# Packing the buffers of an encoder kernel without padding, and loading a scaled identity instead of computing it

## The reference

```python
DN_ALPHA = (2 * DEPTH) ** 0.25
...
# layer 0:  h = norm(ALPHA * h + mixer(h)); h = norm(ALPHA * h + swiglu(h))
# layer 1:  h = norm(ALPHA * h + mixer(h)); h = norm(ALPHA * h + experts(h))
```

## Time and profile before

| | |
|---|---|
| runs | 1726.48, 1728.03, 1727.89 us; median 1727.89 |
| profiled execution | 1726.48 us, span 1724.6 us from its first to its last instruction |
| PE busy | 1650.9 us, 96% of the span |
| DVE busy | 1353.5 us, 78% |
| ACT busy | 944.0 us, 55% |
| DMA | 444.23 MB, 258 GB/s over the span |
| mean granted clock of TensorE | 0.958 of full speed |

### The profile page before, as it was taken

One profiled execution on the slowest core, in us unless ns is written; L12 is line 12 of the kernel. 1 busy time (PEld: TensorE's weight loads), 2 busy tenths in 40 slices (PEclk: granted clock), 3 DMA queues, 4 the chain that ended last, 5 costly groups with the idle time before them and its releaser, 6 DMA issues.

```text
span 1724.6 us, 18678 instructions
## 1 busy us (share of the span) xinstructions
PE 1650.9 (96%) x7674; PEld 1306.7 (76%) x7674; DVE 1353.5 (78%) x1443; ACT 944.0 (55%) x943; POOL 56.4 (3%) x39
## 2 busy tenths in 40 slices
PE   6998989999999998899999999999999999999995
PEld 4665748988858764788888888888888888888883
DVE  6879456765665945598898998888988989888996
ACT  4312315654310232477777776777777767777772
POOL 0111000000011100000000000000000000000000
PEclk9978989999998978799999999999999999999997
DMA  7221152743433114598988998998989989989870
GB/s 311 98 98 49 74 212 86 270 182 147 173 145 147 49 73 182 208 371 344 375 351 339 372 353 346 366 362 337 364 348 354 361 356 356 360 330 374 350 305 26
DMA packets 40459, 444.23 MB, mean 258 GB/s; under 512 B 4400, under 2 KB 4528, under 8 KB 7216
## 3 DMA queue, kind: packets, MB, share of 16 engines
q1 hardware_dynamic: 39216, 438.78, 65.2%
q10 hardware_dynamic: 1152, 4.19, 0.6%
HBM read 437.71 MB, written 5.24 MB: 257 GB/s over the span
## 4 chain that ended last, share of the span: by engine, by line
PE 84%; DVE 10%; ACT 4%; issue 1%; DMA 0%; DVEq 0%; SPq 0%; ACTq 0%
PE bank L1075 33%; PE bank L1096 15%; PE bank L981 7%; PE bank L583 4%; PE bank L990 3%; PE bank L800 3%; PE bank L587 3%; PE bank L1039 2%; PE bank L753 1%; PE bank L1083 1%; DVE ring_lo L1962 1%; DVE ring_lo L2086 1%; ACT ex_up_hi L1353 1%; PE bank L726 1%; PE bank L1059 1%
## 5 line engine op out<-in xcount | busy, mean ns | idle before, releaser
L1962 DVE TENSOR_TENSOR ring_lo<-ring,ex_up_hi 128x2048 fp32r<-128x2048 f32 x224 | 512.8, 2290 | 50.9 <-ACT ex_up_hi L1353 50.7
L1353 ACT ACTIVATE ex_up_hi<-ring 128x2048 fp32r<-128x2048 f32 x224 | 429.1, 1916 | 115.7 <-PE bank L1075 108.0
L1075 PE MATMUL bank<-ex_up_hi,ex_x_hi 128*128 128x512 f32 x896 | 363.0, 405 | 3.7 <-DVE ring_lo L1962 3.7
L1075 PE MATMUL bank<-ring_lo,ex_x_hi 128*128 128x512 f32 x896 | 350.6, 391 | 0.0
L1075 PE MATMUL bank<-ex_up_hi,ex_x_lo 128*128 128x512 f32 x896 | 349.7, 390 | 0.0
L2086 DVE TENSOR_TENSOR ring_lo<-ring,ex_w_hi 128x2048 fp32r<-128x2048 f32 x112 | 255.5, 2282 | 1.4 <-ACT ex_w_hi L1449 1.4
L1449 ACT ACTIVATE ex_w_hi<-ring 128x2048 fp32r<-128x2048 f32 x112 | 213.4, 1905 | 0.0
L1075 PEld LDWEIGHTS bank<-ex_up_hi,ex_x_hi 128*128 128x128 f32 x896 | 168.3, 188 | 40.9 <-DVE ring_lo L1962 10.8
L1075 PEld LDWEIGHTS bank<-ring_lo,ex_x_hi 128*128 128x128 f32 x896 | 168.2, 188 | 36.2
L1075 PEld LDWEIGHTS bank<-ex_up_hi,ex_x_lo 128*128 128x128 f32 x896 | 168.8, 188 | 30.5
L1096 PE MATMUL bank<-ex_w_hi,ex_mid_hi 128*128 128x512 f32 x448 | 174.4, 389 | 2.1 <-DVE ex_mid_lo L2080 2.1
(11 more groups left out here) (316 smaller groups left out, 2187.7 us busy)
## 6 DMA issues: line engine op xcount, KB each, us to landing
ring<-moe SPq DMA_DIRECT2D x112, 2048.0 KB, 7.6
ring<-moe SPq DMA_DIRECT2D x112, 1024.0 KB, 7.6
ring<-ffn SPq DMA_DIRECT2D x11, 3072.0 KB, 10.9
win<-w_in SPq DMA_DIRECT2D x12, 2048.0 KB, 8.6
win<-w_out SPq DMA_DIRECT2D x4, 2048.0 KB, 10.4
lnb<-ln SPq DMA_DIRECT2D x4, 1024.0 KB, 6.1
tab<-yT ACTq DMA_DIRECT2D x8, 512.0 KB, 5.6
pr<-par SPq DMA_DIRECT2D x2, 1728.0 KB, 12.2
```

Source lines behind the costliest of these rows:

```text
L1075: ins = mm(b[:, :], ex_x[x % 2][x_][:, k, :], (ex_up_hi, lo)[w_][:, k, :], start=(k == 0 and m == 0), stop=(k == KT - 1 and m == 2))
L1353: act(ex_up_hi[:, HS * q:HS * (q + 1), :], wt[:, HS * q:HS * (q + 1), :], ACT.Copy).then_inc(e_uh, 1)
L1962: tt(ring_lo[s][:, half], ring[s][:, half], hi.bitcast(F32), ALU.subtract).then_inc(e_ul, 1)
```

## The change

The paddings go: `columns()` returns the exact widths, `vo` its exact width, and the assert is dropped. The fields of `par` are put in another order. A field `alpha` (ALPHA times the identity, 128 columns) is appended to `const`, ACT's instruction that made it is removed, and PE's two L520 matmuls per tile read the field instead; in place of `d_id` they wait for the load of the constants' second piece, which holds it.

```diff
-    return out, -(-at // LINE) * LINE
+    return out, at
...
-    ("m0", 2), ("nm0", 2), ("halfpi", 1), ("lower", NE * NE)])
+    ("m0", 2), ("nm0", 2), ("halfpi", 1), ("lower", NE * NE), ("alpha", P)])
...
-    ("s5_c", 2 * 16 * 32), ("s5_b", 512), ("glu", 512), ("hy_w3", 1024), ("hy_w12", 64), ("gate_w", KT * 16),
-    ("router", KT * NE), ("gate_b", 16), ("a_re", 16), ("a_im", 16), ("log_dt", 16), ("conv", 10 * 4), ("hy_bias", 4),
-    ("ret_gn", 2), ("ml_gn", 2), ("s5_d", 2), ("hy_b1", 1), ("hy_b2", 1), ("hy_freq", 1)])
+    ("conv", 10 * 4), ("hy_bias", 4), ("ret_gn", 2), ("ml_gn", 2), ("s5_d", 2),
+    ("a_re", 16), ("a_im", 16), ("log_dt", 16), ("s5_c", 2 * 16 * 32), ("s5_b", 512), ("glu", 512),
+    ("hy_w12", 64), ("hy_w3", 1024), ("hy_b1", 1), ("hy_b2", 1), ("hy_freq", 1),
+    ("gate_w", KT * 16), ("gate_b", 16), ("router", KT * NE)])
...
-            assert name in ("lead", "over") or place_of[name] % (4 * LINE) == 128
...
-        vo = sb("vo", [P, -(-TT * VO // LINE) * LINE])
+        vo = sb("vo", [P, TT * VO])
...
-        alpha_id = sc[:, 768:768 + P]
...
-                        pe.wait_ge(d_id, 1)
+                        pe.wait_ge(s_pos, 16)
                         for hf in range(2):
-                            mm(bank[2 * t + hf][:, :], alpha_id, h[:, t, hf * 512:(hf + 1) * 512],
+                            mm(bank[2 * t + hf][:, :], K("alpha"), h[:, t, hf * 512:(hf + 1) * 512],
...
-                    act(alpha_id, ident, ACT.Copy, scale=ALPHA).then_inc(d_id, 1)
...
+    put("alpha", ALPHA * np.eye(P))
```

More of the change, by code:

```diff
@@ L59 @@
 HT_BANK = (0, 4, 0, 0)
-LINE = 64
 MAGIC = 12582912.0
@@ L173, in trunk @@
         qkT = ret[:, 1024:2048].rearrange("p (f n) -> p f n", f=4)
-        vo_t = vo[:, 0:TT * VO].rearrange("p (t c) -> p t c", t=TT)
+        vo_t = vo[:, :].rearrange("p (t c) -> p t c", t=TT)
         v65 = vo_t[:, :, 0:VW].rearrange("p t (a c) -> p t a c", a=H)
@@ L314, in trunk @@
         e_yl = sem("ex_y_split")
-        d_half, d_id = sem("ffn_down_first_tokens"), sem("ffn_scaled_identity")
+        d_half = sem("ffn_down_first_tokens")
         s_out = sem("out_written")
```

## The result

The changed kernel takes 1744.89 us (median of 4 runs, 1740.84 to 1745.97), the one before 1727.96 us (median of 4, 1726.48 to 1730.51). The quotient of these medians is 1.0098; the ratio estimated from all executions (those of the changed kernel lie between 1740.45 and 1749.75 us) is 1.0103, with a 95% interval of 1.0081 to 1.0126. So the change makes the kernel slower by 1.0%, some 17 us. The profiled execution took 1744.89 us, its span is 1743.1 us, and the mean granted clock is 0.959 (before 0.958).

A forecast was written before the change was run, and what follows sets the result against it. PE, busy for 96% of the span, was taken as the bound. Terms of 0 (ACT), 0 (new wait), 0 to 0.1 (loads) and 0 (moved buffers) gave +0.1 us, a median of 1728.0 us, range 1724 to 1738.

The forecast's parts named there:

- ACT's instruction: Removing ACT's 0.31 us copy at 249.78 us only lengthens ACT's idle time there: 0.
- The loads: Larger second piece of constants, smaller par, on SP's queue: 0 to 0.1 us, within 0.36 us of slack.
- Rival D: Loads of par take twice their 4.15 us, ACT's first use starts 3.8 us later: 1731.8 us, chance 0.03.
- The moved buffers: Operands of nearly all long instructions start at new offsets; bounded between nothing and 65 us, taken as 0.
- 3, 1 and 0 ns: Costs read from the earlier trace for operands off a boundary on DVE, ACT and PE.
- 13 ns: Time of a PE matmul beside its columns; the upper end let it come twice for each moved operand's matmul.
- The range from 0 to 65 us: Bounds on the moved buffers' cost to PE; the upper end is 5000 matmuls times 13 ns.
- Rows 7 to 9: Earlier trace rows of DVE, ACT and short PE matmuls with offset operands, taken as showing no such price.
- Rival B: Faster: buffers no longer share one offset, so collisions end; 2.1 to 4.2 us gained, about 1724, chance 0.08.
- Rival A: Slower: moved operands cost PE part of a line, 1.7 ns each; 1730.7 or 1738 us, chance 0.25 with its far end.
- 5000 matmuls: Count with moved operands: 4032 in the experts, plus 704 ups and 264 downs in the dense stage.
- C, the clock: Small shifts change the mixers' time at 1.2 GHz by 3.5 us: 1724.4 or 1731.5, chance 0.03 each side.

The follow-up runs named there:

- e8: Whole change, but cst and vo placed behind sc and pr given 3456 columns, so all long-matmul operands start at 128 modulo 256: 1727.68 us, ratio 0.9998.
- e4: Kernel before with 32 bytes of space ahead of the ring slots, so every tensor is at 160 modulo 256: 1729.02 us against 1729.6.
- e2: Kernel before with only a 32-byte dummy ahead of pr, so pr and everything behind it are at 160 modulo 256: 1741.45 us, ratio 1.0082.
- e5: Kernel before with pr, hT, ret and vo moved to 160 modulo 256, all else at 128: 1728.93 us against 1728.35.
- e9: Kernel before with only uT, and so the stationary ex_mid_lo, moved to 160 among the experts' buffers: 1737.73 us against 1727.51.
- e10: Layout of e6 with matmuls reordered, those streaming high parts first, then those streaming ring_lo: 1741.45 us against 1727.51 for the kernel before.
- e6: Kernel before with 32 bytes ahead of cst: ring, h and lnb at 128 modulo 256, all else at 160: 1744.24 us against 1728.35.
- e11: Layout of the kernel before with the matmul order of e10, as a control: 1722.33 us against 1727.51.

## Why the prediction was wrong

**ACT's instruction: 0, right.** ACT's timeline after shows only longer idle time around the same work, 7.74 and 4.39 us against 7.75 and 4.20 in the earlier trace rows:

```profile
253.53 2.00 ACT L1359 ACTIVATE ff_up_hi<-ring 128x1024 fp32r<-128x1024 f32 x2 [7.74 <-PE bank L798]
259.93 0.60 ACT L1144 ACTIVATE ff_x_hi<-bank 128x512 fp32r<-128x512 f32 x1 [4.39 <-PE bank L512]
```

**The loads: 0 to 0.1 us, right as far as it can be told.** ACT's first use of `par` comes at 17.75 us, 0.96 us earlier than in the earlier trace rows:

```profile
17.75 0.21 ACT L1162 ACTIVATE small<-pr 128x16 f32<-128x16 f32 x1
```

and e8, with the same loads, isn't slower. Rival D (the rows of `par` land late) is refuted by both. The Trainium skill's rule on transfers that begin off a boundary (DMA: Bandwidth & Descriptors, How a descriptor splits into AXI transactions) let me expect at most a few per cent of one load; the rows show no delay that would bear it out.

**The moved buffers: the step that failed.** "Of these I take 0, because the rows nearest to it on all three engines (3, 1 and 0 ns) are far nearer to nothing than to 13 ns." The runs show 5.3 ns on each of the 4032 long matmuls. The range from 0 to 65 us held that; the value taken from it did not. There are three faults in the step.

First, the quantity was wrong. I asked what an operand costs that starts off a boundary of its own, and the rows of the trace answered that well: nothing. e4 confirms it, with every tensor moved and no time lost. But the cost hangs on two operands at once, and no row of the kernel before could show it, since there all tensors had one offset. Rows 7 to 9 therefore didn't weigh between 0 and 13 ns at all; I used their silence as evidence. Rival B had the fact ("all tensors start at the same place modulo 256") and read it with the wrong sign: for 512 columns sameness was the fast case. For 256 columns it was right: in the kernels that move `ff_x_hi` they gain the 2 us that rival B priced, though not in the kernel after, where they stay at one offset.

Second, the places were wrong. I added up the columns and got 4 or 8 bytes past a multiple of 16; the allocation rounds to 32 bytes. Rival A, the part of a line of 16 bytes, so had no object. The Trainium skill (SBUF — State Buffer, Door 1: The DMA port swizzle) speaks of such lines, and no operand of the long matmuls starts inside one, in any kernel here, so no run tests that rule for them.

Third, the count was off with it. I had 5000 matmuls, the dense stage's 704 and 264 among them. The 704 aren't moved against their weights at all, since `hT` comes to lie at 128 again: L979 takes 286 ns as L981 did. The 264 downs of the dense stage have 512 columns and a moved stationary operand, and at the full clock they start 232.7 ns apart instead of 229.2: 264 x 3.5 ns = 0.9 us of the 1.4 us by which the stage is longer. The 4032 carry the cost.

"L1075 and L1096 still start 0.227 us apart, a chunk still takes 8.41 us" was the sign I named for being right, and it is the sign by which it fell. The sign for rival A, downs with `ex_w_hi` further apart than those with `ring_lo`, didn't appear either (232.4 and 232.9 against 233.7). **C, the clock,** moved both mixers by a few us in opposite directions, and the sum by about -1 us. It explains none of the 17 us.

The Trainium skill (SBUF — State Buffer, A bandwidth-pool intuition that's wrong) gives TensorE a second, independent read port for weight loads, and (SBUF: two separate sides) says that within the engines' side only the pair shared by VectorE and GpSimd causes contention. For the engines among each other the runs agree: DVE's and ACT's durations don't change with the layout (2290 ns before and after for DVE's up halves, 2282 and 2282 for its down halves, 1916 and 1915 for ACT's up halves), and in the kernel after the spacing is 232.5 ns over the 74 intervals in which both idle, against 233.1 over all. Independence of TensorE's own two reads the runs don't bear out: under a weight load from another offset the stream takes as much as 238 ns instead of 226.7. That it is the two reads that meet is my reading and not shown; it wouldn't explain by itself why 256 columns get shorter.

What is shown: the slowdown is the layout's (e2, e8); it hangs on the relative place (e4), between the streamed operand and the stationary one loaded under it (e5 from either side, e9); its effect lasts over some matmuls that follow (e10 against e6). What stays open: why, and why 256-column matmuls gain by what costs the 512-column ones. Whether 256 bytes are the period I didn't separate from a larger one beyond this: in the kernel before, tensors whose places differ by odd multiples of 256 run at the fast spacing. Differences under 32 bytes weren't tried, as the allocation yields none. Why the downs lose only 2 to 3 ns at +64 is not explained.

## What to carry to other kernels

When matmuls of 512 columns follow one another without a gap, the place of a buffer is part of their cost: keep what is streamed and what is loaded as stationary at one offset modulo 256 bytes (seen here for the fast float32 form alone; at 256 columns it was the other way, by 2 ns), and read the places from the built program, not from the sum of columns. A buffer whose width changes moves everything behind it, so an edit to a table of constants can slow down a loop that never reads it. A price that the trace can't show isn't zero: when it multiplies 4032 instructions on the bounding engine, ask whether the rows vary the quantity at all, and if they don't, keep the chance of the upper half.

## What the runs showed of the hardware

- 512-column matmuls in the fast float32 form start 226.7 ns apart when streamed operand and the stationary one being loaded share their offset modulo 256, and about 233 ns apart (227 to 240, often 235, 232, 235, 231 in turn) when they don't. The weight load takes 188 ns either way.
- 256-column matmuls go the other way: 119.8 ns apart at one offset, 117.9 (e2) where the streamed `ff_x_hi` is moved.
- After a disturbance the spacing needs some matmuls to fall back to 226.7 ns: mostly five behind the transposes of the kernel before (nine in some 25 chunks), and one to eight behind the mismatches of e10. A mismatch on every third matmul thus costs nearly as much as one on all (8.60 against 8.61 us a chunk).
- The time spent at 1.2 GHz, nearly all outside the experts, varies from run to run by up to some 24 us whatever the layout (137.5 to 161.1 us in all), which moves the total by several us. A single run's total misled in e5 and e11, where the stage didn't.
